# A mixture-of-experts decoder step: the fullest expert's overflow moved into its own wide block, and the two smallest experts in blocks of 32 slots

## The chip, the cores and the metric

One core of a Trainium2 chip runs the whole step as one program. The metric is the device time of one execution in microseconds; the median of the runs of a kernel counts. The kernel before took 1341.24 us (three runs, 1340.64 to 1341.29).

## The reference, cut to what matters

A step of 536 rows (16 meta tokens, 512 prompt tokens, 8 sample tokens): a mixer (state-space groups and a short convolution), a residual, a norm, then a top-4-of-32 mixture of experts, a residual and a final norm. The changed part is the mixture:

```
logits = x2 @ w_router + b_router
top_v, top_i = top_k(logits, 4);  gates = softmax(top_v)
for each expert e, for the tokens that chose it:
    gu = x @ w_gate_up[e] + b_gate_up[e]          # 1024 -> 2 x 1024
    gate = min(gu[:, :1024], 7);  up = clip(gu[:, 1024:], -7, 7)
    h = gate * sigmoid(1.702 * gate) * (up + 1)
    y = h @ w_down[e] + b_down[e]                 # 1024 -> 1024
out[token] = sum over its 4 experts of gate_weight * y
```

All of it is in 32-bit floats. Every expert has 8 MB of gate and up weights and 4 MB of down weights, read once from memory. Which tokens an expert gets is known only at run time.

## The kernel before

**Stages.** The mixer and the router take the first fifth of the time. Then comes the expert loop, 33 blocks at positions 0 to 32, and the final norm. The router sorts the experts by their number of tokens (`by_size`, lines 1663 to 1676) and gives each position an expert (`pos_rank`, lines 1254 to 1264). Expert 0 always comes first, as its weights are loaded before the router is done. The 16 next in size get *wide* blocks, the 15 smallest *small* ones.

**Wide block (128 slots).** `wide`, line 2221. Each weight row block (a *unit*, 128 x 1024) is split by ScalarE (`split`, line 1988) and VectorE (line 2436) into a high and a low part, and TensorE (`products`, line 2185) makes three products of each with 128-wide weights: 24 units, 16 for gate and up, 8 for down. Up to six split units are held ahead (`SLOTS`).

**Small block (64 slots).** `small`, line 2344. TensorE takes the weights unsplit in 32-bit form, two column groups of 64 side by side (`small_gate_up`, line 2299, `small_down`, line 2309).

**Quarter block (32 slots).** Four column groups of 32 side by side (`quarter_gate_up`, line 2275, `quarter_down`, line 2289). Before, it served two things: the part of the fullest expert beyond 128 tokens, and an overflow loop (`over`, line 2376) for anything beyond the experts' capacities, which runs at the end only if needed.

**Order.** Two wide blocks, three pairs of small and wide, a wide one (position 8), three pairs (9 to 14), small 15, then position 16 (`TOP`), the fullest expert, wide, with its overflow block 17 (`REST_OF_TOP`) woven in by `wide_with_rest`, line 2243; three pairs (18 to 23), wide 24, three pairs (25 to 30), and two small blocks 31 and 32. In `wide_with_rest` TensorE makes the overflow's eight gate-up groups all at once before unit 18 and its eight down groups after unit 23.

**Weights.** One expert's weights fit in the buffers `ring_lo` (gate and up) and `w_out` (down). The sync queue (SP) loads the next expert in eight pieces (`weight_load`, line 1083), each as soon as the old piece is done with. Behind a wide block that is when VectorE has split it (`load_behind_wide`, line 1840, piece j after 4, 8, 14, 16, 18, 20, 22 and 24 splits); behind a small or quarter block when TensorE's products have used it (`load_behind_small`, line 1846). Each block's bias rows go ahead of its weights in the same queue (lines 1830 to 1838). The lines for block 16 and what follows:

```
1866         load_behind_small(expert_at(sp, TOP), TOP, TOP_SMALL - 1)
1867         bias_rows_small(expert_at(sp, REST_OF_TOP), REST_OF_TOP)
1868         load_behind_small(expert_at(sp, TOP + 2), TOP + 2, TOP_SMALL, True)
```

**Tokens.** VectorE makes a one-hot matrix of an expert's slots (`pick`, line 2410), TensorE turns it into token numbers and gate weights (`select`, line 2164), and the GpSimd queue gathers the rows (`gather`, line 1900), adds the results to `token_sums` in memory (`scatter`, line 1908) and waits for that to land (`added`, line 1916), all in one hand-written order (lines 1941 to 1984). TensorE transposes the gathered tokens (line 2172), ScalarE copies them back (`take_x`, `take_x_small`, `take_x_quarter`, lines 1998 to 2009), and `take_y` (line 2021) copies a block's result with its gate weights.

Of the kernel before, what the change touches and what calls it, by code (L numbers as in the profile page):

```python
# [23 lines left out]
P = 128  # L24
D = 1024
KD = D // P
# [26 lines left out]
REST_OF_TOP = TOP + 1  # L53
SECOND_EXTRA = TOP + 2 + 2 * PAIRS[2]
# [3 lines left out]
RUNS = (2, FIRST_EXTRA + 1, TOP + 2, SECOND_EXTRA + 1)  # L58
SMALLS = (0, PAIRS[0], PAIRS[0] + PAIRS[1] + 2, PAIRS[0] + PAIRS[1] + PAIRS[2] + 2)
WIDES = (2, PAIRS[0] + 3, PAIRS[0] + PAIRS[1] + 4, PAIRS[0] + PAIRS[1] + PAIRS[2] + 5)  # L60
TOP_WIDE, TOP_SMALL = WIDES[2] - 1, SMALLS[2] - 1
LAST_SMALL = sum(PAIRS) + 3
# [1033 lines left out]
def bias_load_small(eng, scratch, tb, e, c):  # L1096

    src = scratch["bias"].rearrange("e (f h) r (u n) -> e h u r f n", f=2, u=2)[e, c // 2, c % 2]
    return eng.dma_start(tb["bias"][32 * c:32 * c + 3, :].rearrange("r (f n) -> r f n", f=2), src)
# [9 lines left out]
def router(nc, a, scratch, stack, sb, sem, bank, keep, mid, tb):  # L1109
# [70 lines left out]
    e = keep["loop"]  # L1180
    TILES = [NT - 1] + list(range(NT - 1))
    Q = NT - 1
    keep["bd_sb"] = sem("bd_sb")
# [52 lines left out]
    def _(pool):  # L1236
# [10 lines left out]
        for run, n in enumerate(PAIRS):  # L1247
            pairs = pos_rank_i[:, RUNS[run]:RUNS[run] + 2 * n].rearrange("p (i a) -> p a i", a=2)
            g.iota(pairs[:, 0], pattern=[[1, n]], base=SMALL_RANK + SMALLS[run] - run // 2, channel_multiplier=0)
            g.iota(pairs[:, 1], pattern=[[1, n]], base=WIDES[run] + 1 - run // 2, channel_multiplier=0)  # L1250
        g.iota(pos_rank_i[:, FIRST_EXTRA:FIRST_EXTRA + 1], pattern=[[0, 1]], base=WIDES[1], channel_multiplier=0)
        g.iota(pos_rank_i[:, TOP - 1:TOP], pattern=[[0, 1]], base=SMALL_RANK + TOP_SMALL - 1, channel_multiplier=0)
        g.iota(pos_rank_i[:, TOP:TOP + 2], pattern=[[0, 2]], base=1, channel_multiplier=0)
# [264 lines left out]
    def _(dve):  # L1518
# [142 lines left out]
        def positions():  # L1661
# [9 lines left out]
            done(v.tensor_scalar(cap[:, 1:2], by_size[:], 1.0, float(S_SLOTS // Q_SLOTS), ALU.is_equal, ALU.add))  # L1671
# [72 lines left out]
def experts(nc, a, out, scratch, stack, sb, sem, bank, keep, mid, tb, landed):  # L1744
# [26 lines left out]
    gate_cur = buf("gate_cur", [P, 2])  # L1771
    ssf = keep["pcol"][:, 0:3 * NT].rearrange("p (a i) -> p a i", a=3)
# [8 lines left out]
    def total(q):  # L1781
# [4 lines left out]
        "w_used sel clip sig h hT_psum h_hi h_lo "  # L1786
        "y_sb y_stored y_out y_free curd turns".split())}
    s.update(keep["loop"])
    block = stack.enter_context(nc.Block())
# [39 lines left out]
    def _(sp):  # L1829
# [5 lines left out]
        def bias_rows_small(e, q):  # L1835
            sp.wait_ge(s["bias_used"], q)
            for c in range(4):
                bias_load_small(sp, scratch, tb, e, c).then_inc(t["bias_in"], 16)
# [58 lines left out]
    def _(pool):  # L1897
        pool.sem_inc(s["y_out"], 1)

        def gather(q, parts=1):  # L1900

            pool.wait_ge(s["idx"], q + 1)
            pool.sem_inc(s["turns"], 1)
# [4 lines left out]
        def scatter(q, side, parts=1):  # L1908

            pool.wait_ge(s["y_sb"], q + 1)  # L1910
            pool.sem_inc(s["turns"], 1)
# [4 lines left out]
        def added(q):  # L1916
            pool.wait_ge(s["y_stored"], 16 * q + 16)
            pool.sem_inc(s["y_out"], 1)

# [21 lines left out]
        def pair(run, i, side, extra=False):  # L1941
# [4 lines left out]
            gather(q + 2, 1 if extra else 2)  # L1946
# [5 lines left out]
        pair(0, PAIRS[0] - 1, 0, True)  # L1952
# [5 lines left out]
        gather(TOP)  # L1958
        added(TOP - 2)
        scatter(TOP - 1, 1, 2)  # L1960
        gather(REST_OF_TOP, 4)
        added(TOP - 1)
        gather(TOP + 2, 2)
        scatter(TOP, 0)
        added(TOP)
        scatter(REST_OF_TOP, 1, 4)
        with pool.Fori(0, PAIRS[2] - 1) as i:
            pair(2, i, 0)
        pair(2, PAIRS[2] - 1, 0, True)
        gather(SECOND_EXTRA + 1, 2)  # L1970
        added(SECOND_EXTRA - 1)
        scatter(SECOND_EXTRA, 0)
        with pool.Fori(0, PAIRS[3]) as i:
            pair(3, i, 1)
        gather(FINAL, 2)
        added(FINAL - 2)
        scatter(FINAL - 1, 1, 2)
# [3 lines left out]
        scatter(FINAL, 0, 2)  # L1981
# [5 lines left out]
    def _(act):  # L1987
# [43 lines left out]
        def wide(q, side, lq, next_parts, loads):  # L2031
# [10 lines left out]
            if next_parts == 2:  # L2042
# [9 lines left out]
        def wide_with_rest(q, side, lq, sq, loads):  # L2052

            for j in range(SLOTS, UNITS):
                if j == 17:
                    gated(q, lq, 0)
                elif j == 20:
# [3 lines left out]
                elif j == 22:  # L2061
                    take_x_quarter(q + 1)
# [3 lines left out]
            act.wait_ge(s["h"], 2 * q + 2)  # L2066
            quarter_hidden(q + 1, sq, bank[1])
            act.wait_ge(s["w_used"], UNITS * lq + UNITS)
            take_y(q, side, [4, 5], [512, 512])
            take_x_small(q + 2)  # L2070
            act.wait_ge(t["s_used"], t0["s_used"] + LOADS * sq + LOADS)
            take_y(q + 1, 1 - side, [3], [256])

        def small(q, side, sq, loads, lq=None, next_parts=4):
# [9 lines left out]
            if lq is not None:  # L2084
                split(loads + 1, lq, 0)
                split(loads + 1, lq, 1)
                take_x(q + 1)
                split(loads + 1, lq, 2)
                split(loads + 1, lq, 3)
            elif next_parts == 2:  # L2090
                take_x_small(q + 1)
            act.wait_ge(t["s_used"], t0["s_used"] + LOADS * sq + LOADS)
            take_y(q, side, [4], [512])
            if lq is None:
                if next_parts == 4:
                    take_x_quarter(q + 1)
            else:
                split(loads + 1, lq, 4)
                split(loads + 1, lq, 5)
# [7 lines left out]
        def quarter(q, sq):  # L2107
            quarter_hidden(q, sq, bank[5])
            act.wait_ge(t["s_used"], t0["s_used"] + LOADS * sq + LOADS)
            take_y(q, 0, [4], [256])  # L2110
# [8 lines left out]
        def pair(run, i, side, extra=False):  # L2119
# [533 lines left out]
```

## Time and profile before

| | |
|---|---|
| median of three runs | 1341.24 us |
| the profiled execution: span of its instructions | 1339.6 us |
| TensorE matmuls busy | 1240.5 us, 93% of the span |
| VectorE busy | 828.6 us, 62% |
| ScalarE busy | 610.9 us, 46% |
| GpSimd busy | 145.4 us, 11% |
| memory traffic | 457.44 MB, 341 GB/s over the span |
| mean granted TensorE clock | 0.976 |

The profiled execution is one of the program; around its span lies what the runs' time counts besides. Busy shares are means over the whole program. The slices of the page are a fortieth of the span each, 33.5 us, numbered from 0: the expert loop starts in slice 8 and ends in slice 39. In the rows of the timeline a time in brackets is how long the engine stood idle before the row, and the name behind it is what released it. "SPq" is the sync engine's queue, and its rows are issues of transfers, not the transfers themselves; a row that covers several issues starts with the first and lasts to the last, waits included. Instructions of 32-bit matmuls count double: a product of 32-bit operands is two instructions.

### The profile page before, as it was taken

How to read it: one execution, taken by the hardware profiler on the slowest of the kernel's cores; microseconds unless marked ns; L12 is line 12 of the kernel's file. 1: busy time of each engine (PE TensorE's matmuls, PEld its weight loads, DVE VectorE, ACT ScalarE, POOL GpSimd, SP SyncE). 2: the span in 40 equal slices, each digit the busy share in tenths (PEclk: the TensorE clock that was granted, in tenths of full speed). 3: DMA queues.
4: the chain of work that ended last, by engine and by line, in shares of the span. 5: the costliest groups of instructions: out<-in, count | busy, mean ns of one | idle time of the engine just before them, and what ended most of it. 6: DMA issues, size and time to landing. Idle time of an engine off the chain costs nothing.

```text
span 1339.6 us, 18513 instructions
## 1 busy us (share of the span) xinstructions
PE 1240.5 (93%) x6184; PEld 802.4 (60%) x6185; DVE 828.6 (62%) x1352; ACT 610.9 (46%) x826; POOL 145.4 (11%) x165
## 2 busy tenths in 40 slices
PE   7999999899999999999999999799999999999992
PEld 5888864477574747747464656364747747464630
DVE  3896758699392838837464656183839837464613
ACT  4111242478273636736354544172737735353502
POOL 9100012010001010010101100100010010101100
PEclk9999999989999999999999999899999999999997
DMA  9610177399999999999999994999999999999994
GB/s 321 90 39 1 39 248 314 131 333 410 360 415 411 420 412 418 409 401 416 409 417 401 403 399 189 405 420 416 419 412 419 400 372 420 404 414 398 400 401 151
DMA packets 67355, 457.44 MB, mean 341 GB/s; under 512 B 15916, under 2 KB 19508, under 8 KB 34520
## 3 DMA queue, kind: packets, MB, share of 16 engines
q1 hardware_dynamic: 56344, 435.28, 79.6%
q0 software_dynamic: 10944, 21.30, 6.7%
q8 instruction: 38, 0.62, 0.2%
q14 instruction: 29, 0.24, 0.0%
HBM read 440.26 MB, written 23.50 MB: 346 GB/s over the span
## 4 chain that ended last, share of the span: by engine, by line
PE 40%; DMA 20%; DVE 11%; issue 4%; ACT 3%; POOL 0%; DVEq 0%; SPq 0%; POOLq 0%; ACTq 0%
PE bank L2192 23%; DMA ring_lo<-in_w_gate_up 14%; PE bank L2302 11%; DVE w_lo L2439 8%; DMA ymix<-ffn_in,idx_next 5%; ACT w_hi L1996 2%; PE bank L2313 2%; DMA token_sums<-ymix,row_cur 1%; PE bank L2175 1%; PE bank L2182 1%; DVE cmix L2457 1%; DVE h_lo L2452 1%; DVE cmix L2460 1%; PE bank L2278 1%; ACT ymix L2026 0%
## 5 line engine op out<-in xcount | busy, mean ns | idle before, releaser
L2439 DVE TENSOR_TENSOR w_lo<-ring_lo,w_hi 128x1024 fp32r<-128x1024 f32 x271 | 316.0, 1221 | 95.7 <-ACT w_hi L1996 93.9
L1996 ACT ACTIVATE w_hi<-ring_lo 128x1024 fp32r<-128x1024 f32 x271 | 271.4, 1053 | 83.7 <-DMA ring_lo<-in_w_gate_up 61.3
L2302 PE MATMUL bank<-ring_lo,x_s 128*64 128x512 f32 x960 | 216.1, 597 | 3.1 <-DMA ring_lo<-in_w_gate_up 2.6
L2192 PE MATMUL bank<-w_hi,x_hi 128*128 128x512 f32 x544 | 176.1, 405 | 8.3 <-DVE x_lo L2445 6.0
L2192 PE MATMUL bank<-w_lo,x_hi 128*128 128x512 f32 x544 | 170.8, 396 | 0.0
L2192 PE MATMUL bank<-w_hi,x_lo 128*128 128x512 f32 x544 | 170.3, 395 | 0.0
L2439 DVE TENSOR_TENSOR w_lo<-w_out,w_hi 128x1024 fp32r<-128x1024 f32 x136 | 161.5, 1219 | 5.1 <-ACT w_hi L1996 5.1
L1996 ACT ACTIVATE w_hi<-w_out 128x1024 fp32r<-128x1024 f32 x136 | 140.8, 1055 | 31.4 <-PE bank L2192 31.2
L2302 PEld LDWEIGHTS bank<-ring_lo,x_s 128*64 128x64 f32 x960 | 65.0, 137 | 122.3 <-issue 116.6
L1912 POOL DMA_INDIRECT token_sums<-ymix,row_cur x33 | 56.1, 1699 | 741.7 <-ACT ymix L2026 704.8
L2192 PEld LDWEIGHTS bank<-w_hi,x_hi 128*128 128x128 f32 x544 | 101.3, 194 | 38.0 <-issue 13.6
L2192 PEld LDWEIGHTS bank<-w_lo,x_hi 128*128 128x128 f32 x544 | 104.0, 191 | 22.5
L2192 PEld LDWEIGHTS bank<-w_hi,x_lo 128*128 128x128 f32 x544 | 103.9, 191 | 22.5
L2313 PE MATMUL bank<-w_out,h_s 128*64 128x512 f32 x480 | 113.0, 603 | 0.0
L2465 DVE TENSOR_SCALAR cmix<-bank 128x256 f32<-128x256 f32 x30 | 12.7, 425 | 161.1 <-ACT cmix L2081 161.1
L2192 PE MATMUL bank<-w_hi,h_hi 128*128 128x512 f32 x272 | 89.0, 409 | 6.5 <-DVE h_lo L2452 6.5
L2192 PE MATMUL bank<-w_lo,h_hi 128*128 128x512 f32 x272 | 84.5, 392 | 0.0
L2192 PE MATMUL bank<-w_hi,h_lo 128*128 128x512 f32 x272 | 84.1, 391 | 0.0
L2419 DVE TENSOR_REDUCE sel<-bank 128x2 f32<-128x6 f32 x33 | 5.4, 165 | 120.6 <-PE bank L2168 119.0
L2081 ACT ACTIVATE cmix<-bank 128x256 f32<-128x256 f32 x30 | 11.5, 383 | 148.1 <-PE bank L2302 148.1
L2026 ACT ACTIVATE ymix<-bank,gate_cur 128x512 f32<-128x512 f32 (+1 forms) x50 | 32.2, 679 | 97.9 <-PE bank L2192 75.3
L562 PE MATMUL bank<-hT,ring_lo 128*128 128x272 f32 x224 | 69.7, 393 | 0.0
(445 smaller groups left out, 1406.5 us busy)
## 6 DMA issues: line engine op xcount, KB each, us to landing
ring_lo<-in_w_gate_up SPq DMA_DIRECT2D x128, 2048.0 KB, 18.6
w_out<-in_w_down SPq DMA_DIRECT2D x128, 1024.0 KB, 20.6
ring_lo<-in_w_in SPq DMA_DIRECT2D x3, 2048.0 KB, 21.8
w_out<-in_w_out SPq DMA_DIRECT2D x2, 2048.0 KB, 9.4
x<-in_x_prompt SPq DMA_DIRECT2D x6, 512.0 KB, 11.7
bias<-bias_rows SPq DMA_DIRECT2D x132, 3.0 KB
ring_lo<-in_w_in SPq DMA_DIRECT2D x2, 1024.0 KB, 9.9
token_sums<-x SPq DMA_DIRECT2D x4, 512.0 KB
```

Of the source, the lines that this page charges most:

```text
L562: last = nc.tensor.matmul(hi[:, 0:REST], w_k(ORDER[n], k), hT[:, k, HALF:TOK], start=(k == 0), stop=(k == KD - 1))
L1912: nc.gpsimd.indirect_dma_start(row_parts["acc", parts], bass.IndirectOffsetOnAxis(ap=row_cur[:, side:side + 1].bitcast(U32), axis=0), yo[: ...
L1996: nc.scalar.activation(high(j), raw(j), ACT.Copy).then_inc(s["w_hi"], 1)
L2026: last = nc.scalar.activation(yo[:, h * 512:h * 512 + n], bank[b][:, 0:n], ACT.Copy, scale=gate_cur[:, side:side + 1])
L2175: last = nc.tensor.transpose(bank[6 + k // 4][:, (k % 4) * P:(k % 4 + 1) * P], xg[:, k * P:(k + 1) * P], ident[:])
L2182: last = nc.tensor.transpose(bank[6 + half][:, k * P:(k + 1) * P], h_sb[:, c:c + 2 * P - 1:2], ident[:])
L2192: last = nc.tensor.matmul(bank[b + u][:], v[:, k, :], part(j)[:, u, :], start=(j == 16 and first), stop=(k == KD - 1 and part is high and ...
L2278: last = nc.tensor.matmul(bank[0][32 * c:32 * c + 32, :], x_s[:, k % 2, 32 * (k // 2):32 * (k // 2) + 32], gu[:, k, :, c // 2, 256 * (c % ...
L2302: last = nc.tensor.matmul(bank[2 * half][64 * u:64 * u + 64, :], x_s[:, k % 4, 64 * (k // 4):64 * (k // 4) + 64], gu[:, k, :, half, 256 * ...
L2313: last = nc.tensor.matmul(bank[4][64 * u:64 * u + 64, :], h_s[:, 2 * half + c, 64 * u0:64 * u0 + 64], ring_hi[:, k, 512 * u:512 * u + 512] ...
L2439: v.tensor_tensor(low(j), raw(j), high(j).bitcast(F32), ALU.subtract).then_inc(s["w_lo"], 1)
L2452: v.tensor_tensor(h_lo[:, c, :].rearrange("p k t -> p (k t)"), bank[6 + half][:], h_hi[:, c, :].rearrange("p k t -> p (k t)").bitcast(F32) ...
```

## The change

1. Position 17 goes away. The overflow of the fullest expert is picked during small block 15 (`rest_slots`, `select_rest`), gathered right after block 16's tokens (`gather_rest`) and transposed at the end of block 15. `take_x_rest` copies the transposed tokens after ScalarE's work for block 15, and block 16 waits for it. In block 16 the overflow's gate-up groups come one at a time after units 0, 1, 4, 5, 8, 9, 10 and 11, its down groups after units 18 to 23. Its own buffers lie in the tile `x`, and it has its own semaphores, spent ones of earlier stages.
2. The loads of the next expert wait behind block 16 for both the splits and the overflow's groups (`load_behind_rest`).
3. The overflow's scatter goes ahead of block 16's, and GpSimd waits for its landing.
4. The two smallest experts (positions 30 and 31 now) become quarter blocks, with a capacity of 32 tokens each; the capacity table gets one instruction more.
5. The positions behind 16 move down by one; one more pair of run 3 is written out, as its last wide block prepares a quarter block.

The diff, cut to its core:

```diff
+REST_AFTER = {0: 0, 1: 1, 4: 2, 5: 3, 8: 4, 9: 5, 10: 6, 11: 7}
+REST_DOWN_AFTER = {18: (0,), 19: (1, 2), 20: (3,), 21: (4,), 22: (5,), 23: (6, 7)}
...
-            done(v.tensor_scalar(cap[:, 1:2], by_size[:], 1.0, float(S_SLOTS // Q_SLOTS), ALU.is_equal, ALU.add))
+            done(v.tensor_scalar(cap[:, 1:2], by_size[:], 1.0, 1.0, ALU.is_equal, ALU.add))
+            done(v.scalar_tensor_tensor(out=cap[:, 1:2], in0=by_size[:], scalar=QUARTER_RANK - 0.5, in1=cap[:, 1:2], op0=ALU.is_lt, op1=ALU.add))
...
+        def load_behind_rest(e, q, lq):
+            bias_rows_small(e, q)
+            for j in range(LOADS):
+                sp.wait_ge(s["w_lo"], UNITS * lq + (4, 8, 14, 16, 18, 20, 22, 24)[j])
+                if j % 4 < 3:
+                    sp.wait_ge(r["used"], r0["used"] + 3 * (j // 4) + j % 4 + 1)
+                else:
+                    done = ("sums", "y_psum")[j // 4]
+                    sp.wait_ge(r[done], r0[done] + 1)
+                weight_load(sp, a, keep, mid, e, j).then_inc(landed[j], 16)
...
-        load_behind_small(expert_at(sp, TOP), TOP, TOP_SMALL - 1)
-        bias_rows_small(expert_at(sp, REST_OF_TOP), REST_OF_TOP)
-        load_behind_small(expert_at(sp, TOP + 2), TOP + 2, TOP_SMALL, True)
+        e_top = expert_at(sp, TOP)
+        sp.wait_ge(keep["bd_added"], 16 * NT)
+        for c in range(4):
+            bias_load_small(sp, scratch, bias_rest, e_top, c).then_inc(r["bias"], 16)
+        load_behind_small(e_top, TOP, BEFORE_TOP)
+        load_behind_rest(expert_at(sp, TOP + 1), TOP + 1, TOP_WIDE)
...
         gather(TOP)
+        gather_rest()
         added(TOP - 2)
         scatter(TOP - 1, 1, 2)
-        gather(REST_OF_TOP, 4)
+        gather(TOP + 1, 2)
         added(TOP - 1)
-        gather(TOP + 2, 2)
+        scatter_rest()
         scatter(TOP, 0)
-        added(TOP)
-        scatter(REST_OF_TOP, 1, 4)
...
         # ScalarE in block 16
+                if j == 17:
+                    rest_gated()
                     gated(q, lq, 0)
+                elif j == 19:
+                    take_rest_h()
...
+        small(TOP - 1, 1, BEFORE_TOP, TOP, TOP_WIDE)
+        take_x_rest()
+        wide_with_rest(TOP, 0, TOP_WIDE, TOP + 1)
...
         # TensorE in block 16
             pe.wait_ge(s["x_lo"], lq + 1)
+            pe.wait_ge(r["x_s"], r0["x_s"] + 1)
+            set_bias_rest()
...
+                if j == 15:
+                    rest_h_transposes()
...
                 if j == 18:
+                    pe.wait_ge(r["h_s"], r0["h_s"] + 1)
                     h_transposes(q, 1)
-                    pe.wait_ge(t["x_s"], t0["x_s"] + sq + 1)
-                    for k in range(KD):
-                        quarter_gate_up(k)
...
                 products(lq, j)
+                if j in REST_AFTER:
+                    rest_gate_up(REST_AFTER[j])
+                for k in REST_DOWN_AFTER.get(j, ()):
+                    rest_down(k)
...
         # TensorE at the end
-        small(FINAL - 1, LAST_SMALL - 1, FINAL - 1, expert_at(pe, FINAL), 2)
-        small(FINAL, LAST_SMALL, FINAL, over_expert(pe, 0), 4)
+        quarter(FINAL - 1, LAST_SMALL - 1, FINAL, expert_at(pe, FINAL))
+        set_bias_quarter(FINAL)
+        quarter(FINAL, LAST_SMALL, FINAL + 1, over_expert(pe, 0))
```

## Rows read from the trace of the kernel before

**Rows 1.** The page, busy share of the 16 DMA engines by slice, in tenths

```profile
DMA  9610177399999999999999994999999999999994
```

**Rows 2.** Busy time by window: us, PE, PEld, DVE, ACT, POOL, PEclk, DMA, GB/s

```profile
813.00:824.00 11.00, 11.00 (x65) 7.32 (x67) 9.59 (x11) 6.07 (x8) 0.00 (x0) 0.87 0.01 2
```

**Rows 3.** Timeline of the sync queue, blocks 16 to 18

```profile
791.89 27.82 SPq L1099 DMA_DIRECT2D bias<-bias_rows  x8
...
823.42 5.83 SPq L1089 DMA_DIRECT2D ring_lo<-in_w_gate_up  x4
...
838.60 2.92 SPq L1089 DMA_DIRECT2D w_out<-in_w_down  x4
...
846.55 11.22 SPq L1089 DMA_DIRECT2D ring_lo<-in_w_gate_up  x4
```

**Rows 4.** The chain of waits: start, us, what

```profile
346.86 2.73 PE bank L2302 x12
...
764.90 2.73 PE bank L2302 x12
...
1267.00 2.73 PE bank L2302 x12
```

**Rows 5.** Timeline of PE, blocks 16 to 18: start, us, what, idle before

```profile
812.22 1.11 PE L2182 MATMUL bank<-ident,cmix 128*128 128x128 f32 x4 [2.28 <-DVE cmix L2460]
...
821.29 5.36 PE L2278 MATMUL bank<-ring_lo,x_s 128*32 128x512 f32 x48
...
826.79 1.92 PE L2278 MATMUL bank<-ring_lo,x_s 128*32 128x512 f32 x16
...
828.65 0.74 PE L2192 MATMUL bank<-w_hi,h_hi 128*128 128x512 f32 x2
...
837.33 3.66 PE L2292 MATMUL bank<-w_out,h_s 128*32 128x256 f32 x64
...
842.35 2.80 PE L2302 MATMUL bank<-ring_lo,x_s 128*64 128x512 f32 x12 [0.43 <-ACT x_s L2005]
...
869.31 1.97 PE L2175 MATMUL bank<-ident,ymix 128*128 128x128 f32 x8 [8.04 <-DMA ymix<-ffn_in,idx_next]
```

**Rows 6.** DMA queues, 347 to 765 us, then 842 to 1267: packets, MB, share

```profile
q1 hardware_dynamic: 15137, 162.11, 91.9%
...
q0 software_dynamic: 3360, 8.36, 8.1%
...
q1 hardware_dynamic: 15778, 167.41, 93.8%
...
q0 software_dynamic: 3504, 6.29, 6.1%
```

**Rows 7.** Tile ymix on GpSimd, 765 to 780 us: issue to landing

```profile
DMA to landing us min/median/max: 12.0/14.0/16.1
```

**Rows 8.** Timeline of ACT, block 16

```profile
791.32 5.99 ACT L1996 ACTIVATE w_hi<-ring_lo 128x1024 fp32r<-128x1024 f32 x6 [0.17 <-ACT ymix L2026]
...
832.03 0.38 ACT L2105 ACTIVATE h_s<-bank 128x256 f32<-128x256 f32 x1 [2.78 <-PE bank L2286]
```

**Rows 9.** Timeline of PE, block 32; tile w_out, its last loads and their landing

```profile
1301.96 4.51 PE L2302 MATMUL bank<-ring_lo,x_s 128*64 128x512 f32 x20 [2.65 <-DMA ring_lo<-in_w_gate_up]
...
1315.30 0.44 PE L2175 MATMUL bank<-ident,ymix 128*128 128x128 f32 x2
...
L1089 SPq DMA_DIRECT2D w_out<-in_w_down x4: 332/333/333, 1283.7 to 1290.5; - x4
...
DMA to landing us min/median/max: 20.7/20.8/21.6
```

**Rows 10.** Timeline of PE, wide block 8 and the block behind it

```profile
536.38 0.62 PE L2192 MATMUL bank<-w_hi,x_hi 128*128 128x512 f32 x2
...
572.23 1.08 PE L2302 MATMUL bank<-ring_lo,x_s 128*64 128x512 f32 x4
```

**Rows 11.** DMA queues, 1316 to 1322 us, the last scatter

```profile
q0 software_dynamic: 144, 0.09, 14.1%
```

More of the change, by code:

```diff
@@ L1180, in router @@
     e = keep["loop"]
+    keep["rest"] = {"onehot": (s["consts"], 1), "sel_psum": (s["first_psum"], 1), "sel": (s["mix_var"], 1), "row": (s["mix_root"], 1),
+                    "idx": (s["wr"], 1), "x_in": (sem("rest_x_in"), 0), "xT": (s["count_psum"], 1), "x_s": (s["xg_clear"], 1),
+                    "sums": (s["upto_psum"], 1), "clip": (s["extra"], 1), "sig": (s["tabs"], 1), "h": (s["held"], 1),
+                    "hT": (s["rank_psum"], NT), "h_s": (s["exp"], NT), "y_psum": (s["x_var"], NT), "y_sb": (s["x_root"], NT),
+                    "stored": (sem("rest_stored"), 0), "used": (s["mask"], NT), "bias": (s["wr_in"], 32)}
     TILES = [NT - 1] + list(range(NT - 1))
     Q = NT - 1
+    keep["spent"].update({"turns": (s["lg"], NT), "clip": (s["sub"], NT), "sel": (s["gates"], NT)})
     keep["bd_sb"] = sem("bd_sb")
@@ L1785, in experts @@
     s = {n: sem("e_" + n) for n in (
-        "w_used sel clip sig h hT_psum h_hi h_lo "
-        "y_sb y_stored y_out y_free curd turns".split())}
+        "w_used sig h hT_psum h_hi h_lo "
+        "y_sb y_stored y_out y_free curd".split())}
     s.update(keep["loop"])
+    r = {n: v[0] for n, v in keep["rest"].items()}
+    r0 = {n: v[1] for n, v in keep["rest"].items()}
     block = stack.enter_context(nc.Block())
@@ L1939, in _, with pair @@
         scatter(1, 1)
-        def pair(run, i, side, extra=False):
+        def pair(run, i, side, next_parts=2):
             q = RUNS[run] + 2 * i
@@ L1980, in _ @@
         more = more_blocks(pool)
-        scatter(FINAL, 0, 2)
+        scatter(FINAL, 1, 4)
         added(FINAL)
@@ L2210, in set_bias_quarter, with set_bias_rest @@
             last.then_inc(s["bias_used"], 1)
+        def set_bias_rest():
+            pe.wait_ge(r["bias"], r0["bias"] + 64)
+            nc.tensor.transpose(bank[7][:, 0:P], ident[:], ident[:])
+            for c in range(4):
+                nc.tensor.matmul(bank[7][32 * c:32 * c + 32, :], tb["one_b"][32 * c:32 * c + 3, 0:1].to_broadcast([3, 32]),
+                                 bias_rest[32 * c:32 * c + 3, :], start=True, stop=False)
         def set_bias_small(q):
@@ new lines, in wide_with_rest, with rest_gate_up @@
+                for k in REST_DOWN_AFTER.get(j, ()):
+                    rest_down(k)
+        def rest_gate_up(k):
+            for c in range(4):
+                last = nc.tensor.matmul(bank[7][32 * c:32 * c + 32, :], xs_rest[:, k % 2, 32 * (k // 2):32 * (k // 2) + 32],
+                                        gu[:, k, :, c // 2, 256 * (c % 2):256 * (c % 2) + 256], start=False, stop=(k == KD - 1))
+            if k == KD - 1:
+                last.then_inc(r["sums"], 1)
+            elif k % 2 == 1:
+                last.then_inc(r["used"], 1)
@@ new lines, in rest_h_transposes, with rest_down @@
+        def rest_h_transposes():
+            pe.wait_ge(r["h"], r0["h"] + 1)
+            for c in range(2):
+                last = nc.tensor.transpose(bank[7][:, c * P:(c + 1) * P], h_rest[:, c:c + 2 * P - 1:2], ident[:])
+            last.then_inc(r["hT"], 1)
+        def rest_down(k):
+            for c in range(4):
+                last = nc.tensor.matmul(bank[1][32 * c:32 * c + 32, 0:256], hs_rest[:, k % 2, 32 * (k // 2):32 * (k // 2) + 32],
+                                        ring_hi[:, k, 256 * c:256 * c + 256], start=(k == 0), stop=(k == KD - 1))
+            if k == KD - 1:
+                last.then_inc(r["y_psum"], 1)
+            elif k % 2 == 1:
+                last.then_inc(r["used"], 1)
```

318 lines of the change are left out of this document (170 added, 148 removed).

## The prediction

> **What bounds the kernel now.** I read the busy share of the transfer engines by slice first. From slice 11 on they are full (9) but for one slice of 4 in the middle and the end [rows 1]. In that stage TensorE (PE) also has work nearly all the time, so the question at each place is which of the two waits. The hole is at block 16, the fullest expert's wide block, together with its overflow block 17: for 11 us nothing moves (share 0.01) [rows 2]. The sync queue (SP) shows why. It sends the bias rows of block 17 and then stands, and the next expert's gate and up weights leave only at 823.42, when the overflow block has used chunk after chunk of the old ones; the down weights leave at 838.60 [rows 3]. The reader is to see that the transfers stop not for want of bandwidth, but because the buffer (one expert deep) is held by products that come late.
>
> Second, what such a hole costs. The chain of waits gives the starts of small blocks: 346.86 (block 2), 764.90 (block 15) and 1267.00 (block 31) [rows 4], and the PE timeline gives 842.35 for block 18 [rows 5]. Blocks 2 to 14 and blocks 18 to 30 have the same order of wide and small blocks. The first stretch takes 418.04 us, the second 424.65. The weight queue (q1) moved 162.11 MB in the first and 167.41 MB in the second, the gather and scatter queue 8.36 and 6.29 MB [rows 6]: block 18 begins with 5.3 MB of its weights still on the way, and that debt lengthens the stretch.
>
> **Part 1, small block 15.** It gains the picking of the overflow's slots (one selection, 0.2 us on PE), two transposes (0.4), and a second gather right behind that of block 16, on the same GpSimd queue. A scatter and a gather there landed 12.0 and 16.1 us after issue [rows 7]. The second gather may land with the first or some 4 us behind; it is a quarter row wide, so I take 0.5, ends 0 and 4. Block 15's last product, now about 790.4, comes at 791.5. Four bias loads more on SP are issued while SP waits for PE anyway; they cost nothing here. Uncovered they would hold the weight loads back by under 3 us (four loads with their waits took 2.92 [rows 3]).
>
> **Part 2, the start of block 16.** PE now waits for the copy of the overflow's transposed tokens (`take_x_rest`), which ScalarE (ACT) does after all of block 15's work. ACT's copy of y ends at 791.15, and six splits follow in 5.99 us, 1.0 each [rows 8]. Two of these stand ahead of the new copy. So from 791.5: y copy 0.8, two splits 2.0, copy 0.4, hand-over 0.3, then the bias products 0.5, and the first unit starts at 795.5 instead of about 790.4. Behind this wait stand all 24 units. PE is idle for 3.5 us. An idle of 2.28 us in this same block came before four transposes of 1.11 us in all [rows 5], and the mean granted clock of the 11 us from 813 is 0.87 [rows 2]: of these 2.9 us stood at the lower level, 1.2 GHz, with the microsecond before it nearly 4, which gives away half of that. An idle of 2.65 before 1301.96 was followed by 20 matmuls in 4.51 us, full speed [rows 9]. So it can go either way: 0 or 1.9, and I take 1.9, since this idle is longer than both.
>
> **Part 3, inside block 16.** A wide block alone takes 35.85 us from its first unit to the next block's (536.38 to 572.23) [rows 10], the usual wait for h included. The overflow's gate-up products are as many as before, 48 in 5.36 and 16 in 1.92 [rows 5]; the difference of the two, 3.44 for 32, makes 0.1075 each, 7.0 for 64 with the gaps. The down products are 64 in 3.66 [rows 5], 3.5 net. The overflow's transposes of h cost 0.4. What is new is that these come in 14 small groups between units. A switch costs: 16 matmuls from 826.79 end by that pitch at 828.51, and the next unit starts at 828.65 [rows 5], 0.14. With 28 switches that is 3.9. Bounds: 0, if the pipeline hides them, and 28 times 0.3, 8.4.
>
> The Trainium skill (TensorEngine Tiling (Array Packing), Key Properties) says that changing the tiling mode, unlike changing only the tile, drains TensorE. That speaks against this change, which alternates 128-wide and 32-wide column tiles. The row above agrees with it, at 0.14 us. The page gives no figure of its own; with no drain the sum would be 3.9 us lower.
>
> Sum: 795.5 + 1.9 + 35.85 + 7.0 + 3.5 + 0.4 + 3.9 = 848.1, when the next small block starts, against 842.35. PE is 5.7 us later, since the old form hid the overflow's latencies well and had no wait at the start. VectorE's (DVE) one-hot, reductions and swiglu for the rest are few and short, and hide behind the inserted products. If that cover is gone, they show at unit 16, where ACT's `take_rest_h` waits for PE with splits 19 and on behind it, as one more wait like that of 2.28 us.
>
> **Part 4, the transfers.** The first three weight loads can go after units 1, 5 and 9, the fourth after the last gate-up product, near 821; nothing then stands idle for long. But the down loads wait for groups after units 19, 20, 22 and 23, from about 836 to 848. So the hole isn't closed, it is split: some 10 us without transfers before those loads. What is gained is that at 848.1 nearly nothing is outstanding, where it was 5.3 MB. The next load goes 4.2 us after the small block's start (846.55 against 842.35) [rows 3, 5].
>
> How long is the stretch to the last pair then? Two rows bound it. Blocks 2 to 14 began with an empty queue: 418.04; they moved 2.07 MB more of gathers and scatters, 5.1 us at 409 GB/s, so 413 to 418. From the other side, the stretch as it was less 5.3 MB at 409 GB/s (13.0 us) gives 411.7, and with 4.2 us of empty queue ahead 415.9. I take 415.5. The block that takes the place of 31 starts at 848.1 + 415.5 = 1263.6, 3.4 us earlier than 1267.00. On the other side stands the GpSimd queue: the overflow's scatter waits for its landing ahead of block 16's scatter and the next gather. In the old form that gather was late too, PE stood 8.04 us for it [rows 5] with transfers going on; I put 0.5 (0 to 5).
>
> **Part 5, the two last blocks at 32 slots.** PE's work falls by about half, but the last two are paced by the transfers. Before, the last load landed at 1290.5 + 21.6 = 1312.1, 45.1 us after 1267.00; the last gate-up chunk at 1301.96, 35 after; the last product came at 1315.3, 48.3 after [rows 9]. Landings keep their distance (the queue is full). With 32 slots, after the last gate-up chunk: two k-steps 1.9 to 3.7 (the low clock is likely between chunks), hand-over through ACT and DVE about 3 (ACT's h copy began 3.3 us after the gate-up products ended at about 828.7 [rows 8]), down 3.5 to 5.6; together about 12, so 47 after the start, and 1.3 earlier than before. It can't be earlier than 46, one chunk's products after the last landing. The y copy is half as wide, 0.3. Sum -1.6, ends -3 and 0. The leaner scatters are left at nothing. The one added VectorE operation in the router stands on the path: +0.3.
>
> **Sum:** -3.4 + 0.5 - 1.6 + 0.3 = -4.2. The profiled span is 1339.6, the median of the runs 1.6 above it; I set the change against 1341.24: **1337.0 us**.
>
> **Rivals.**
> (A) Transfers alone set the pace, so everything saved in the queue comes back: block 17 at 846, stretch 411.7, which is 1257.7, 9.3 early; with 3 at the end 1329. For it: the full shares [rows 1]; against: PE is as full.
> (B) The gain is spent: one more wait of 3 us in block 16 and 418 instead of 415.5 give 1342. For it: 10 us of hole remain.
> (C) Slower. Place: units 12 to 19 of block 16, where PE waits for h, ACT for the rest's transposes, and DVE for ACT's splits, each in its own order. Price: two waits of 2.3 us like the one seen, each followed by 1.9 at the low clock, 8.4 more: block 17 at 856.5, and the end at 1345.4. It decides from a start of block 17 later than about 855.
> (D) The change doesn't hold its capacity: if one of the two smallest experts has over 32 tokens, an overflow block reloads 12.6 MB, 31 us: 1370. Against: the last scatter moved 0.09 MB [rows 11], at 4 KB a token 22 tokens, the smallest expert; the next in order of size would need ten more tokens to break the bound.
>
> **Chances.** Forecast 0.5, A 0.2, B 0.17, C 0.12, D 0.01. A measurement of this kernel tells 0.2% (2.7 us) from no change. The forecast's own spread puts a tenth of it within 0.2%, B gives 0.15 there and the rest slower: faster 0.66, same 0.20, slower 0.14. The range takes in A's end and the mild side of C: 1329 to 1344.
>
> **What would show it.** Step by step: PE idle of 3 to 4 us before block 16's first unit, released by ACT's copy; the next small block at 848 (before 845 I overpriced the switches, after 852 a wait is missing); loads of block 17 leaving from about 801 with a second hole before its down weights; a shorter stretch, 413 to 418; the last product 46 to 48 us after block 30's start. It is wrong if that start comes later than 1267, or if the fourth gate-up load still leaves near 829.

## The result, and the profile after

The changed kernel takes **1347.82 us**, the median of 5 runs (1346.64 to 1348.76); beside it the kernel before took 1341.29 (5 runs, 1340.64 to 1344.44). The ratio is 1.0043, 95% interval 1.0032 to 1.0053: 6.5 us slower, where the forecast was 4.2 us faster with a range of 1329 to 1344. Both the sign and the range were wrong.

First the page of the kernel after: span, granted clock and busy share of the transfers by slice.

```profile
span 1346.5 us, 18538 instructions
...
PEclk9999999889999999999999989989999989999986
DMA  9610176399999999999999996898999999999994
```

The single 4, in slice 24 [rows 1], has become a 6 with an 8 behind it: the transfers do stand less. So the change did what it says, and the profiled span is 6.9 us longer all the same. Where the time went is read from the block starts. The chain of waits of the kernel after (start, us, what) gives that of block 15, the PE timeline those of 17 and of the first block in 32 slots, 30:

```profile
764.79 2.73 PE bank L2399 x12
```

```profile
795.45 0.44 PE L2284 MATMUL bank<-ident 128*128 128x128 f32 x1 [5.31 <-issue]
...
832.80 0.73 PE L2261 MATMUL bank<-w_hi,h_hi 128*128 128x512 f32 x2 [1.89 <-DVE h_lo L2548]
...
852.44 2.79 PE L2399 MATMUL bank<-ring_lo,x_s 128*64 128x512 f32 x12
...
879.39 1.97 PE L2244 MATMUL bank<-ident,ymix 128*128 128x128 f32 x8 [8.02 <-DMA ymix<-ffn_in,idx_next]
...
924.13 2.80 PE L2399 MATMUL bank<-ring_lo,x_s 128*64 128x512 f32 x12
...
1275.01 1.92 PE L2375 MATMUL bank<-ring_lo,x_s 128*32 128x512 f32 x16
...
1321.66 0.44 PE L2244 MATMUL bank<-ident,ymix 128*128 128x128 f32 x2
```

Up to block 15 the kernels agree to 0.2 us [rows 4]. Then: block 16 starts behind an idle of 5.31 us, its unit 16 waits 1.89 for h, block 17 starts at 852.44 (forecast 848.1; its counterpart before 842.35 [rows 5]), PE stands 8.02 us for block 18's tokens, and block 30 starts at 1275.01 (forecast 1263.6; before 1267.00 [rows 4]). From there to the last product it is 46.7 us (forecast 47; before 48.3 [rows 4, 9]). So the loss lies in two places, inside block 16 and in the stretch behind it.

ACT's timeline shows both waits from the other side:

```profile
787.46 2.00 ACT L2045 ACTIVATE w_hi<-ring_lo 128x1024 fp32r<-128x1024 f32 x2 [4.04 <-DMA ring_lo<-in_w_gate_up]
...
793.08 2.00 ACT L2045 ACTIVATE w_hi<-ring_lo 128x1024 fp32r<-128x1024 f32 x2 [0.17 <-ACT ymix L2075]
794.98 0.36 ACT L2133 ACTIVATE x<-bank 128x256 f32<-128x256 f32 x1
...
829.56 0.39 ACT L2109 ACTIVATE x<-bank 128x256 f32<-128x256 f32 x1 [2.38 <-PE bank L2359]
...
830.79 0.59 ACT L2068 ACTIVATE h_hi<-bank 128x512 fp32r<-128x512 f32 x1
```

ACT's splits begin only when the weights have landed (787.46), and from there it works with hardly a gap (0.17 us) until the copy of the overflow's tokens at 794.98; PE starts at 795.45. At unit 16 it stands 2.38 us for the overflow's transposes (`take_rest_h`), with a split and the copy of h behind.

Busy time by window (us, PE, PEld, DVE, ACT, POOL, granted clock, DMA share, GB/s) shows that both waits in block 16 were followed by TensorE at its lower level, 1.2 GHz, all the time in the first of these windows (0.50) and part of it in the second (0.78):

```profile
796.00:800.00 4.00, 4.00 (x14) 2.02 (x14) 1.44 (x2) 0.67 (x1) 0.00 (x0) 0.50 1.03 409
...
832.00:836.00 4.00, 3.20 (x10) 2.56 (x11) 3.97 (x6) 2.81 (x4) 0.00 (x0) 0.78 0.05 20
```

The GpSimd timeline shows why the tokens of block 18 are late. The overflow's scatter goes at 853.82, and block 16's scatter waits 4.72 us for its landing; the gather stands behind both:

```profile
853.82 1.59 POOL L1964 DMA_INDIRECT token_sums<-x  x1 [39.60 <-ACT x L2128]
860.13 1.56 POOL L1944 DMA_INDIRECT token_sums<-ymix,row_cur  x1 [4.72 <-DMA token_sums<-x]
861.99 1.06 POOL L1936 DMA_INDIRECT ymix<-ffn_in,idx_next  x1 [0.30 <-issue]
```

By the view of tile ymix on GpSimd (845 to 885 us) that one gather landed 13.0 to 17.3 us after its issue, the last part at 879.3, where PE went on:

```profile
DMA to landing us min/median/max: 13.0/15.2/17.3
```

The queue of weight loads did as forecast: the gate and up chunks leave from 803.53, and the second hole follows before the down chunks.

```profile
842.22 10.76 SPq L1091 DMA_DIRECT2D w_out<-in_w_down  x4
```

### The profile page after: what moved, and what is told of

It is laid out like the page before. It is cut to its first block, busy times and chain, and to the rows that moved or that the text cites. A ratio compares the mean times of both kernels' runs of the same rounds, so it can differ in the third digit from the quotient of the medians.

```text
span 1346.5 us, 18538 instructions
## 1 busy us (share of the span) xinstructions
PE 1237.5 (92%) x6242; PEld 795.6 (59%) x6243; DVE 828.7 (62%) x1347; ACT 609.8 (45%) x822; POOL 144.3 (11%) x165
## 4 chain that ended last, share of the span: by engine, by line
PE 38%; DMA 20%; DVE 14%; issue 5%; ACT 2%; DVEq 0%; SPq 0%; POOL 0%; ACTq 0%; POOLq 0%
PE bank L2261 21%; DMA ring_lo<-in_w_gate_up 12%; DVE w_lo L2535 10%; PE bank L2399 10%; DMA w_out<-in_w_down 4%; DMA ymix<-ffn_in,idx_next 4%; PE bank L2410 2%; ACT w_hi L2045 1%; PE bank L2244 1%; DVE cmix L2553 1%; PE bank L2251 1%; DVE h_lo L2548 1%; PE bank L2349 1%; DVE cmix L2556 1%; DMA token_sums<-x 0%
## 5 line engine op out<-in xcount | busy, mean ns | idle before, releaser
L2399 PE MATMUL bank<-ring_lo,x_s 128*64 128x512 f32 x832 | 187.3, 597 | 0.0
L2399 PEld LDWEIGHTS bank<-ring_lo,x_s 128*64 128x64 f32 x832 | 56.2, 136 | 102.6 <-issue 100.7
L2410 PE MATMUL bank<-w_out,h_s 128*64 128x512 f32 x416 | 101.8, 623 | 0.0
```

The costliest lines, as they stand in the source:

```text
L2399: last = nc.tensor.matmul(bank[2 * half][64 * u:64 * u + 64, :], x_s[:, k % 4, 64 * (k // 4):64 * (k // 4) + 64], gu[:, k, :, half, 256 * ...
L2410: last = nc.tensor.matmul(bank[4][64 * u:64 * u + 64, :], h_s[:, 2 * half + c, 64 * u0:64 * u0 + 64], ring_hi[:, k, 512 * u:512 * u + 512] ...
```

## The experiments

Theory 1 was that TensorE's own waits around blocks 16 and 17 are on the path; theory 2 that the last two blocks in 32 slots cost time; theory 3 that the transfers alone set the pace. Each kernel is the changed one with the edits named, unless said otherwise. Times are medians, ratios are to the kernel before on the same chip (1341.3 to 1342.0 us there). A comparison with the changed kernel (1347.8) is of medians from different series of runs, good to about 1.5 us. The rows of a kernel are those of one execution, which can lie some us beside its median.

### The overflow's scatter no longer holds back block 18's gather (a_gather)

```diff
         scatter_rest()
+        gather(TOP + 2)
+        pool.wait_ge(r["stored"], r0["stored"] + 16)
         scatter(TOP, 0)
```

(the wait stood at the end of `scatter_rest`; the first turn of the pair loop is written out on GpSimd, without its gather)

> The gather for block 18 is issued between the overflow's scatter and the wait for its landing. Theory 1 (TensorE's idle of 8.0 us in block 17 is on the path): the gather is issued at about 856.5 instead of 862, lands by 872, the idle falls under 2 us, blocks 17 to 18 take 62 to 66 us instead of 71.8, and the time falls by 4 to 7 us to 1341 to 1344. Theory 3 (the transfers alone set the pace from block 17 on, as my forecast had it): the idle falls as well, but the stretch from block 17 to block 30 stays at 422 to 423 us and the time within 1.5 us of 1347.8.

Measured 1343.09 us (12 runs), ratio 1.0006 [0.9997, 1.0015]: 4.7 us less than the changed kernel. GpSimd, then PE:

```profile
855.00 1.03 POOL L1936 DMA_INDIRECT ymix<-ffn_in,idx_next  x1 [1.32 <-DVE idx_next L2526]
```

```profile
850.69 2.79 PE L2405 MATMUL bank<-ring_lo,x_s 128*64 128x512 f32 x12
...
869.55 1.09 PE L2250 MATMUL bank<-ident,ymix 128*128 128x128 f32 x8
...
911.61 2.79 PE L2405 MATMUL bank<-ring_lo,x_s 128*64 128x512 f32 x12
...
1267.91 1.92 PE L2381 MATMUL bank<-ring_lo,x_s 128*32 128x512 f32 x16
```

The eight transposes of block 18's tokens show no idle, and block 17 to 19 takes 60.9 us instead of 71.7 (924.13 in the kernel after). Of these 10.8 us, 5.4 are left at block 30: the stretch is 417.2 instead of 422.6, so half is given back later to the weight transfers: over the stretch ACT waits 29.3 us for gate and up weights, where it waited 14.7 in the kernel after. The profiled execution was the fastest of the twelve (1340.48), so its positions flatter the edit; by the medians the wait for the scatter is on the path and worth 4.7 us, as theory 1 had it.

### The last two blocks back in 64 slots (a_small)

```diff
-QUARTER_RANK = E - 2
+QUARTER_RANK = E
```

(and blocks 30 and 31 in the small form on every engine)

> The changed kernel with its two last experts in 64 slots again: block 16 and all before it are as changed. Theory 1 (the slowdown comes from waits of TensorE around block 16, the 32-slot end is worth about 1.6 us): block 17 starts at about 852.4 and block 30 at 1275 as in the changed kernel, the last product comes 48.3 us after block 30's start instead of 46.7, and the time is 1.6 us above the changed kernel's 1347.8, about 1349.4. Theory 2 (the end in 32 slots is what costs, by its low clock): faster than 1346.

1348.54 us (6 runs), ratio 1.0054 [1.0037, 1.0071]; against the changed kernel this alone can't tell 1.6 us from nothing. The profile has block 30 at 1272.98 and its last transposes, which end the products, at 1321.57, 48.6 us on, against 46.7. Theory 2 needed a time under 1346, so it falls: no cost of the 32 slots shows. What they are worth is measured below.

### The overflow's tokens copied ahead of two splits (a_xrest)

```diff
             take_x(q + 1)
+            if with_rest:
+                take_x_rest()
             split(loads + 1, lq, 2)
```

> ScalarE copies the overflow's transposed tokens right after block 16's tokens, ahead of the y copy and splits 2 to 5. Theory 1 (TensorE's waits around block 16 are on the path): the idle of 5.3 us before block 16 falls to 1 us or nothing, the granted clock does not fall there, block 17 starts at about 847 instead of 852.4, and the time falls by 3 to 5 us, to 1343 to 1345. Theory 3 (the transfers set the pace): block 17 starts earlier, but the stretch behind it grows by as much; time within 1.5 us of 1347.8.

1342.05 us (12 runs), ratio 0.9997 [0.9986, 1.0008]: 5.8 us less than the changed kernel, a little more than the 3 to 5 expected.

```profile
792.69 0.33 PE L2285 MATMUL bank<-ident 128*128 128x128 f32 x1 [1.26 <-DVE x_lo L2542]
...
828.04 0.73 PE L2262 MATMUL bank<-w_hi,h_hi 128*128 128x512 f32 x2 [1.89 <-DVE h_lo L2549]
...
847.71 2.80 PE L2400 MATMUL bank<-ring_lo,x_s 128*64 128x512 f32 x12
```

Block 16 now starts behind an idle of 1.26 us, released by DVE and no more by ACT. In the windows from 788 to 800 us the granted clock is 1.00, so the edit saves the wait and the slow microseconds after it: from block 15's start to block 17's 81.5 us (766.17 in its chain) instead of 87.7. The other two waits stand: 1.89 at unit 16, and 7.88 for block 18's tokens.

### Block 16's h copied ahead of the overflow's (a_hrest)

```diff
-                elif j == 19:
-                    take_rest_h()
                 elif j == 20:
                     take_h(q, 0)
+                    take_rest_h()
```

> ScalarE takes the first half of block 16's h ahead of the overflow's h, so that it does not stand waiting for the overflow's transposes with split 19 and that copy behind it. Theory 1: TensorE's idle of 3.6 us before unit 16 falls under 1.5 us, no fall of the clock behind it, block 17 starts at 848 to 849.5, time 1344 to 1345.5. Theory 3: the stretch behind grows by as much; time within 1.5 us of 1347.8.

1346.29 us (8 runs), ratio 1.0031 [1.0019, 1.0043]: 1.5 us less than the changed kernel, about the precision of that comparison, and less than the 2.3 to 3.8 expected. (The expectation speaks of an idle of 3.6 us before unit 16; the trace shows 1.89.)

```profile
830.87 0.73 PE L2260 MATMUL bank<-w_hi,h_hi 128*128 128x512 f32 x2 [0.18 <-DVE h_lo L2547]
...
848.94 2.79 PE L2398 MATMUL bank<-ring_lo,x_s 128*64 128x512 f32 x12
```

The wait at unit 16 falls from 1.89 to 0.18: the place of `take_rest_h` in ACT's order was its cause. From its first unit (795.70) block 16 takes 53.2 us to block 17, against 56.1 in the kernel after. a_gather says how that splits, as it has the same wait of 1.89 but no fall of the clock behind it: 54.8 us there (795.88 to 850.69). So the wait is worth 1.6 us, and the remaining 1.3 goes with the fall of the clock, which came in one kernel and not in the other.

### All three (a_134)

> The kernel after with all three single edits at once: block 18's gather issued before the wait for the overflow's scatter, the copy of the overflow's tokens ahead of two splits on ScalarE, and the copy of h ahead of the overflow's. Theory 1 (TensorE's waits around blocks 16 and 17 are on the path and independent of each other): the savings add. Singly they gave 4.7, 5.8 and 1.5 us against the kernel after (1347.8), so the sum is 12.0 and the time 1335.8, between 1333 and 1339; block 17 starts at 844 to 846, the idle before block 18's token transposes is under 2 us, and block 30 starts between 1259 and 1264. Rival (what one edit gives back another gives back too, because the weight transfers then set the pace from block 17 on): 1339 to 1342, with waits of TensorE on weight landings taking the place of those removed.

1334.17 us (5 runs), ratio 0.9941 [0.9928, 0.9955]: 7.1 us faster than the kernel before, 13.6 below the changed one, where the single savings sum to 12.0. They add, as theory 1 had it, and no wait of TensorE of that size takes their place. PE:

```profile
793.06 0.73 PE L2267 MATMUL bank<-w_hi,x_hi 128*128 128x512 f32 x2
...
826.12 0.73 PE L2267 MATMUL bank<-w_hi,h_hi 128*128 128x512 f32 x2 [0.18 <-DVE h_lo L2554]
...
844.20 2.80 PE L2405 MATMUL bank<-ring_lo,x_s 128*64 128x512 f32 x12
...
1261.52 1.92 PE L2381 MATMUL bank<-ring_lo,x_s 128*32 128x512 f32 x16
```

### The same cure in the kernel before (b_gather)

```diff
         scatter(TOP, 0)
+        gather(TOP + 3)
         added(TOP)
         scatter(REST_OF_TOP, 1, 4)
```

(to the kernel before; a third column of `row_cur` and `gate_cur` for block 18 lets VectorE pick block 19's slots before block 16's scatter has landed, and the first turn of the pair loop is written out on GpSimd, ScalarE and VectorE)

> The kernel before, with the same cure for its own late gather: block 19's tokens are gathered ahead of the wait for block 16's scatter (a third pair of row and gate columns lets the slots be picked that early). Before, TensorE stood 8.0 us for them. Theory H (in the kernel before that idle was covered, because the weights of the following block were still on the way behind 5.3 MB of debt): the idle goes and waits for weights take its place, and the time stays within 1 us of 1341.9. Theory V (the idle was on the path before, too, and the change only kept it): 4 to 6 us faster, 1336 to 1338.

1342.25 us (11 runs), ratio 1.0006 [0.9997, 1.0015]: no gain, though the idle of 8.04 us [rows 5] is gone. This is the experiment that names the forecast's error. PE of the kernel before with that edit, where a wait for the halves of x comes instead:

```profile
870.54 1.22 PE L2200 MATMUL bank<-w_hi,x_hi 128*128 128x512 f32 x2 [4.58 <-DVE x_lo L2453]
```

Block 20 starts 67.1 us after block 18 (909.25 and 842.11) instead of 70.7, and of these 3.6 us 0.8 are left at block 31. What x waits for stands on ACT's timeline: it splits the next weights first, and they have not landed. The same kernel, then the kernel before, then the kernel after:

```profile
865.76 2.00 ACT L2002 ACTIVATE w_hi<-ring_lo 128x1024 fp32r<-128x1024 f32 x2 [5.32 <-DMA ring_lo<-in_w_gate_up]
```

```profile
865.97 2.00 ACT L1996 ACTIVATE w_hi<-ring_lo 128x1024 fp32r<-128x1024 f32 x2 [5.29 <-DMA ring_lo<-in_w_gate_up]
871.31 1.09 ACT L2001 ACTIVATE x_hi<-bank 128x512 fp32r<-128x512 f32 x2 [3.34 <-PE bank L2175]
```

```profile
870.67 1.99 ACT L2045 ACTIVATE w_hi<-ring_lo 128x1024 fp32r<-128x1024 f32 x2
881.39 1.08 ACT L2050 ACTIVATE x_hi<-bank 128x512 fp32r<-128x512 f32 x2 [8.73 <-PE bank L2244]
```

Before, PE's 8 us lay mostly over ACT's wait of 5.29 us for weights that came late anyway; only then does ACT stand 3.34 us more for the tokens. After, the weights are there, ACT splits them without a wait and then stands 8.73 us for the tokens: the 8 us are bare. Later blocks take part of a cure back in both kernels, as ACT's waits for gate and up weights over the whole stretch show: 29.8 us before and 34.7 with the cure, 14.7 after and 29.3 with it. In the kernel before that eats the gain, in the kernel after half of it. The earlier loads had taken away the cover of a wait that the trace showed already.

### The overflow's down products two by two (a_1347)

```diff
-REST_DOWN_AFTER = {18: (0,), 19: (1, 2), 20: (3,), 21: (4,), 22: (5,), 23: (6, 7)}
+REST_DOWN_AFTER = {18: (0, 1), 19: (2, 3), 20: (4, 5), 21: (6, 7)}
```

(with the three edits; on ScalarE `take_y` of block 16 now also waits for the block's own last products, as the overflow's last group no longer comes behind them)

> The same three edits, and the overflow's eight down groups after units 18 to 21 instead of 18 to 23, so that the down weights of block 17 may leave some units earlier. Theory 1 (products set the pace around block 16, the transfer hole before the down loads is slack): within 1 us of the kernel with the three edits. Rival (the remaining hole of some 10 us before the down loads is what the stretch still pays for): the loads leave 3 to 5 us earlier and the time falls by 2 to 4 us more.

1332.66 us (5 runs), ratio 0.9933 [0.992, 0.9947]; the interval overlaps that of the three edits alone. The loads of block 17's down weights:

```profile
834.08 9.02 SPq L1091 DMA_DIRECT2D w_out<-in_w_down  x4
```

Neither theory is met to the letter: the time falls by 1.5 us, between "within 1" and "2 to 4". Counted from block 17's start the first of the four loads leaves 11.4 us ahead and the last 2.3 us ahead; with the three edits these are 10.2 us ahead and 0.6 behind (833.98 to 844.76). So the edit brings the loads forward by 1.1 to 2.9 us. They still leave only as the groups end: in a_13478 the loads leave from 829.24, 831.82, 835.34 and 837.92, each 0.2 to 0.3 us behind a pair of groups, while VectorE's last split of the block was done at 829.5. The stretch to block 30 is 416.3 us (845.44 to 1261.78), and 415.9 and 415.7 in the two kernels below that have this edit too, against 417.2 to 417.8 in three without it: 0.9 to 2.1 less. So the hole costs something, as the rival says; what a closed one would give wasn't tried and stays open. One more thing is in this profile: block 16 started behind an idle of 2.57 us and ran its first units at the lower clock, and block 17 starts 1.2 us later than with three edits in spite of fewer changes of form.

### The overflow's gate and up products two by two (a_1348)

```diff
-REST_AFTER = {0: 0, 1: 1, 4: 2, 5: 3, 8: 4, 9: 5, 10: 6, 11: 7}
+REST_AFTER = {1: (0, 1), 5: (2, 3), 9: (4, 5), 11: (6, 7)}
```

(with the three edits)

> The same three edits, and the overflow's eight gate-up groups two by two behind units 1, 5, 9 and 11 instead of one by one behind eight units: 8 changes between wide and narrow column tiles fewer. Theory S (a change of the tile's form costs TensorE about 0.14 us, more where it drains): a unit with two groups behind it takes less than two units with one each, by 0.3 us or more, and block 17 starts 1 to 3 us earlier. Rival (the inserted groups cost their own product time of 0.86 and the rest of the 1.23 us is the loading of their 32-wide weights, which grouping leaves as it is): block 17 starts where it does with the three edits, within 0.4 us.

1333.76 us (5 runs), ratio 0.9939 [0.9925, 0.9952]: not to be told from the three edits by time. The rows do tell. First the three edits, then this kernel:

```profile
799.74 0.61 PE L2267 MATMUL bank<-w_hi,x_hi 128*128 128x512 f32 x2
...
801.10 0.61 PE L2267 MATMUL bank<-w_hi,x_hi 128*128 128x512 f32 x2
...
802.55 1.07 PE L2355 MATMUL bank<-ring_lo,x 128*32 128x512 f32 x8
803.55 0.73 PE L2267 MATMUL bank<-w_hi,x_hi 128*128 128x512 f32 x2
...
805.13 1.07 PE L2355 MATMUL bank<-ring_lo,x 128*32 128x512 f32 x8
```

```profile
813.34 0.74 PE L2267 MATMUL bank<-w_hi,x_hi 128*128 128x512 f32 x2
...
816.33 1.92 PE L2355 MATMUL bank<-ring_lo,x 128*32 128x512 f32 x16
818.18 0.74 PE L2267 MATMUL bank<-w_hi,x_hi 128*128 128x512 f32 x2
```

A unit among units takes 1.36 us (799.74 to 801.10). A unit with one group takes 2.58 (802.55 to 805.13), so a lone group costs 1.22: 0.86 for its eight matmuls at the pitch of the forecast (0.1075) and the rest for the two changes, before and behind it. Two units with a pair of groups take 4.84 (813.34 to 818.18); less 2.72 that is 2.12 for the pair, 0.32 less than two lone ones, for two changes fewer. Four pairs save 1.3 us, and block 16 from its first unit to block 17 (793.37 to 843.12) takes 49.75 us instead of 51.14, 1.4 less for eight changes fewer. So a change of form costs 0.16 to 0.17 us, and theory S holds, a little above the 0.14 of the forecast's row. The Trainium skill (TensorEngine Tiling (Array Packing), Key Properties) says that a change of the tiling mode drains TensorE; the 1.3 to 1.4 us for eight changes fewer agree with it, though they don't show that it is a drain that costs them.

### All five edits (a_13478), and that with 64 slots at the end (a_134782)

> All of the edits together: the three waits cured, the down groups earlier, the gate-up groups in pairs. In the profiles of the kernels with three and four edits, a unit with one group behind it took 2.59 us and one without 1.37, so a lone group costs 1.22; the pair measured 1.85 with 0.24 around it, 0.37 less than two lone ones, four times: block 17 starts 1.5 us earlier. Theory 1 (products set the pace around block 16): 1332 to 1334, between 0 and 2 us below the kernel with the three edits (1334.2). Rival (with TensorE's waits gone the transfers set the pace of all 13 blocks behind): no earlier than 1334.

> The same with the last two blocks back in 64 slots: what the 32-slot end is worth where nothing else differs. By the forecast's part 5: the last product 1.6 us later after its block's start (48.3 against 46.7) and the whole 1.6 slower. Rival (what comes behind the last product gives it back: in the profiles so far 24.3 to 24.6 us from the last product to the end of the span with 64 slots, 24.8 to 26.4 with 32): within 0.7 us of the kernel with the 32-slot end.

With all five edits 1331.81 us (5 runs), ratio 0.9928 [0.9914, 0.9941]: the fastest version of this study, 9.9 us below the kernel before and just under the 1332 to 1334 expected. (It was 2.4 below the kernel with the three edits, so the rival, no earlier than 1334, falls.) With 64 slots 1333.78 (5 runs), ratio 0.9941 [0.9928, 0.9955]. Start of block 30 and the end of the products, first in 32 slots, then in 64:

```profile
1256.49 1.92 PE L2382 MATMUL bank<-ring_lo,x_s 128*32 128x512 f32 x16
...
1302.49 0.44 PE L2251 MATMUL bank<-ident,ymix 128*128 128x128 f32 x2
```

```profile
1257.09 2.80 PE L2423 MATMUL bank<-ring_lo,x_s 128*64 128x512 f32 x12
...
1305.83 0.44 PE L2268 MATMUL bank<-ident,ymix 128*128 128x128 f32 x2
```

46.0 us against 48.7; what follows up to the end of the span gives 0.6 of that back (25.6 us against 25.0). By the medians it is 2.0 us (the intervals overlap by half): nearer the 1.6 forecast than the rival's "within 0.7".

## Why the prediction was wrong

**The sum.** Forecast against the profile before: -3.4 for the start of block 30, +0.5 for the gather, -1.6 at the end, +0.3. Block 30 came 8.0 us later than before (1275.01 against 1267.00, the gather in it) and the end was 1.6 shorter. The forecast missed block 30 by 10.9 (-3.4 + 0.5 against +8.0), and that splits as follows.

**Part 4, the gather behind the overflow's scatter: the step that failed.** "In the old form that gather was late too, PE stood 8.04 us for it with transfers going on; I put 0.5 (0 to 5)." The idle stayed 8.02, as that sentence expects, but it was priced by its change in length and not by what lay under it. Shown by a pair: its cure is worth 4.7 us in the kernel after and nothing in the kernel before, whose weights were late at the same place. That is 5.3 us of stretch (422.6 against 417.2 in a_gather and 417.3 with three edits), 4.8 above the price. Three more kernels keep the wait (a_small, a_xrest, a_hrest) and one more cures it (a_1348): with it the stretch is 421.3 to 423.1 us, without it 417.2 to 417.8. What lay under it is in ACT's rows: 5.29 us of waiting for weights before, none after.

**Part 4, the stretch.** Without that wait it takes 417.2 us in a_gather and 417.3 with three edits against 415.5 forecast, inside 411.7 to 418: 1.8 too little.

**Part 3, the wait at unit 16.** It was named ("they show at unit 16, where ACT's `take_rest_h` waits for PE") and put in rival C, but not in the sum. It cost 1.7 us (1.89 against 0.18), and in this profile a fall of the clock after it. By the chains, of the kernel after and then of that with three edits, units 16 and 17 took 4.29 us where they take 3.02 at the full clock:

```profile
832.80 4.29 PE bank L2261 x12
```

```profile
826.12 3.02 PE bank L2267 x12
```

That is 1.27, and the four transposes behind took 0.77 instead of 0.47: 1.57 in all, together 3.28. The fall is not certain behind such a wait: in a_gather the same 1.89 us were followed by 3.02 us for these units.

**Parts 2 and 3, the rest.** The first unit came at 796.36 (795.5: +0.9). I had counted the copy's turn from block 15's last product; it was ACT's own splits, begun when the weights landed, that set it, and PE's idle was 5.3 instead of 3.5. Part of this is the one execution: with the same code up to here a_small, a_gather and a_hrest show idles of 4.33, 4.11 and 3.95 us and the first unit at 795.0 to 795.9. The slow start cost 1.7 (unit 0 with its group took 4.27 us, 796.36 to 800.63, against 2.59 with three edits), forecast 1.9. The block itself, with products, switches and transposes of h: 50.65 forecast (35.85 + 7.0 + 3.5 + 0.4 + 3.9), and 51.14 measured where no wait and no low clock disturb (793.06 to 844.20): 0.5 too little; 28 changes at 0.16 to 0.17 instead of 0.14 would explain it. So block 17: 848.05 + 0.86 - 0.22 + 0.49 + 3.28 = 852.46, measured 852.44. The products priced by rows were right to half a microsecond; what was missing was a wait and the clock behind it.

**Part 5.** Right: the last product 46.7 us after block 30's start (forecast 47), 1.6 earlier than before, and 2.0 by time in the pair of kernels. Over the eight profiles with 32 slots it was 45.9 to 48.0, so single ones spread by 2 us.

**The rivals.** A is excluded as the pace of the whole: removing waits of PE alone gave 13.6 us. B's mechanism, a hole of 10 us left, is there (DMA share 0.05 from 832 to 836), and its price stays open: bringing the loads forward by 1.1 to 2.9 us made the stretch 0.9 to 2.1 shorter. C named a right place, with two waits of 2.3 us; there was one of 1.9, and block 17 started at 852.44, under its threshold of 855. The slower outcome came from a place to which no rival gave the price: GpSimd's order behind block 16. D did not happen: with over 32 tokens in one of the smallest experts 31 us more would have come.

**The named tests.** The forecast said that a start of block 30 after 1267 would refute it, and so it did; "after 852 a wait is missing" was right to the letter. And the likelihood of 0.66 for faster was too high for a change whose hoped gain of 3.4 us was smaller than one idle of 8 us left uncovered on its way.

## What to carry to other kernels

When a change makes transfers earlier, list every idle of the compute engine that lies over a late transfer now, and charge each at what the transfer will no longer cover, which is at most its bare length (here 4.7 of 8.0 us, as later blocks gave the rest back): an idle shown by the trace is free only while something else is as late, and ACT's row "waits for the weights" right beside it tells which. On an engine with its own fixed order, a short operation for inserted work belongs behind whatever the main line needs from that engine: moving two copies and one gather by a few places turned a change that lost 6.5 us into one that gains 7.1. And a wait of 2 us on TensorE is to be charged with what the clock may take after it: behind the same 1.89 us that was nothing in a_gather and 1.6 us in the kernel after, a_xrest and a_small.

## What the runs showed of the hardware

The clock did not follow the length of the idle alone. After an idle of 5.31 us unit 0 ran at 1.2 GHz (granted 0.50 from 796 to 800), and after one of 2.57 too (a_1347: 0.50 from 792 to 796); after 2.65 in the last block before it was full [rows 9], and even after 3.03 in that of a_134782 (1.00 from 1292 to 1296); so it was after 1.26 and 1.34 at the start of block 16. At unit 16 the same idle of 1.89 us went both ways: granted 0.59 from 828 to 832 in a_xrest, where units 16 and 17 took 4.61 us, and 1.00 from 832 to 836 in a_gather, where they took 3.02.

```profile
828.00:832.00 4.00, 3.96 (x11) 3.10 (x12) 3.92 (x5) 2.05 (x3) 0.00 (x0) 0.59 0.28 119
```

```profile
832.61 3.02 PE bank L2267 x12
```

A scatter that moves little still took its time: the overflow's, 128 pieces of 1 KB, held the next one from 853.82 to 860.13 in the kernel after, 6.3 us, of which GpSimd itself was busy for 1.59. In a_gather, with a gather issued in between, it was 6.6 (852.10 to 858.72).
